# RWKV-7 chunk products merged and partly turned on VectorE, the decay inside the chunk matrices, and expert sums that start from the tokens

## What is computed

```python
def step(S, inp):                       # per head: S is 64 x 64, 8 heads, 256 steps
    r_t, w_t, k_t, v_t, a_t, b_t = inp
    sa = jnp.einsum('bhvk,bhk->bhv', S, a_t)
    S = S * w_t[:, :, None, :] + sa[..., None] * b_t[:, :, None, :] + v_t[..., None] * k_t[:, :, None, :]
    return S, jnp.einsum('bhvk,bhk->bhv', S, r_t)
...
hid = jax.nn.silu(xblk @ w_gate[e]) * (xblk @ w_up[e])      # 1024 -> 512, for each expert e
return hid @ w_down[e]                                      # 512 -> 1024
...
y = jnp.sum(yb[dest].reshape(M, TOP_K, D_) * gates[..., None].astype(yb.dtype), axis=1)
x = x + y
```

## Time and profile before

| | us |
|---|---|
| median of 3 runs | 1618.35 |
| the 3 runs | 1606.52, 1618.35, 1621.35 |
| the profiled execution: time / span | 1607.18 / 1605.4 |
| busy in the span: PE / PEld / DVE / ACT / POOL | 1159.9 / 845.2 / 357.0 / 220.8 / 84.6 |

### The profile page before, as it was taken

The page is one execution under the profiler, slowest core; times in us unless marked ns, Lnnn a source line. Parts: engine busy times, 40 slices in busy tenths (PEclk is TensorE's granted clock), DMA queues, the critical chain, the costliest instruction groups (busy, mean ns, idle before and its releaser), DMA issues.

```text
span 1605.4 us, 37750 instructions
## 1 busy us (share of the span) xinstructions
PE 1159.9 (72%) x16919; PEld 845.2 (53%) x16919; DVE 357.0 (22%) x980; ACT 220.8 (14%) x604; POOL 84.6 (5%) x132
## 2 busy tenths in 40 slices
PE   7988799898998667686656666665666666666565
PEld 4866378554786465475444444444444444444343
DVE  2455124811324514311111111111111011110111
ACT  1044012520014210210000000000000000000000
POOL 1100000000100313000000000000000000000000
PEclk9898899999997768799888888798888888888988
DMA  9740325106020002879999999999999999999997
GB/s 290 280 134 1 93 105 209 27 0 224 1 105 0 3 4 111 363 285 428 429 429 427 429 429 429 428 429 428 429 429 429 429 428 429 429 429 428 428 428 311
DMA packets 68879, 463.30 MB, mean 289 GB/s; under 512 B 14645, under 2 KB 18134, under 8 KB 44246
## 3 DMA queue, kind: packets, MB, share of 16 engines
q1 hardware_dynamic: 64784, 459.76, 69.6%
q10 hardware_dynamic: 4038, 2.69, 0.6%
HBM read 461.38 MB, written 1.05 MB: 288 GB/s over the span
## 4 chain that ended last, share of the span: by engine, by line
DMA 50%; PE 7%; DVE 1%; issue 1%; ACT 0%; POOLq 0%; SPq 0%; DVEq 0%; PEldq 0%; POOL 0%; PEld 0%
DMA weight_slots<-in_exp_w_down_dram 50%; PE bank L2096 4%; PE bank L2087 1%; PE bank L2076 1%; PE bank L2062 0%; PE bank L2055 0%; PE bank L2113 0%; DVE tokens L2285 0%; ACT work_region L2036 0%; SPq L1944 0%; DVE normed_features L2223 0%; DVE normed_tokens L2162 0%; POOLq L1979 0%; PEldq L1923 0%; DVE normed_features L2220 0%
## 5 line engine op out<-in xcount | busy, mean ns | idle before, releaser
L2087 PE MATMUL bank<-weight_slots,work_region 128*32 128x128 f32 x5504 | 200.6, 308 | 128.3 <-DMA weight_slots<-in_exp_w_up_dram 102.9
L2087 PEld LDWEIGHTS bank<-weight_slots,work_region 128*32 128x32 f32 x5504 | 173.9, 124 | 156.7 <-DMA weight_slots<-in_exp_w_up_dram 113.7
L2096 PE MATMUL bank<-weight_slots,work_region 128*32 128x256 f32 x1376 | 112.6, 482 | 90.6 <-DMA weight_slots<-in_exp_w_down_dram 90.6
L2087 PE MATMUL bank<-work_region 128*32 128x128 f32 x2688 | 97.8, 307 | 59.4 <-DMA work_region<-in_exp_w_up_dram 47.6
L2096 PEld LDWEIGHTS bank<-weight_slots,work_region 128*32 128x32 f32 x1376 | 58.1, 133 | 132.4 <-issue 91.8
L2087 PEld LDWEIGHTS bank<-work_region 128*32 128x32 f32 x2688 | 85.0, 124 | 73.2 <-DMA work_region<-in_exp_w_up_dram 53.1
L2036 ACT COPY work_region<-bank 128x256 f32<-128x256 f32 x64 | 23.9, 373 | 607.1 <-PE bank L2096 607.1
L2243 DVE TENSOR_SCALAR work_region<-work_region 128x128 f32<-128x128 f32 x128 | 38.6, 344 | 297.7 <-PE bank L2104 296.6
L2096 PE MATMUL bank<-work_region 128*32 128x256 f32 x672 | 58.8, 505 | 48.4 <-DMA work_region<-in_exp_w_down_dram 46.4
L514 PE MATMUL bank<-weight_slots,normed_features 128*128 128x512 f32 (+2 forms) x256 | 86.8, 499 | 1.9 <-DVE normed_features L700 1.9
L2254 DVE TENSOR_TENSOR work_region<-work_region,bank 128x128 f32<-128x128 f32 x64 | 23.9, 373 | 282.5 <-PE bank L2087 282.5
(11 more groups left out here) (400 smaller groups left out, 1274.6 us busy)
## 6 DMA issues: line engine op xcount, KB each, us to landing
weight_slots<-in_exp_w_up_dram SPq DMA_DIRECT2D x43, 2048.0 KB, 41.0
weight_slots<-in_exp_w_down_dram SPq DMA_DIRECT2D x43, 2048.0 KB, 40.7
weight_slots<-in_exp_w_gate_dram SPq DMA_DIRECT2D x43, 2048.0 KB, 41.7
work_region<-in_exp_w_gate_dram SPq DMA_DIRECT2D x21, 2048.0 KB, 41.7
work_region<-in_exp_w_up_dram SPq DMA_DIRECT2D x21, 2048.0 KB, 41.1
...
```

The lines of the kernel that those rows point to most:

```text
L2087: mm = nc.tensor.matmul(B[bank][BLK * j:BLK * (j + 1), 0:P], xt[u][:, c], w[u][:, c, j * P:(j + 1) * P], start=c == 0, stop=c == KC - 1, t ...
L2096: mm = nc.tensor.matmul(B[7][BLK * j:BLK * (j + 1), 0:256], hidt[u][:, BLK * k:BLK * (k + 1)], w_down[u][:, k, j * 256:(j + 1) * 256], sta ...
```

## The change

In words, and by part:

- The operands a and r now lie side by side (`reads`), so `of_features` multiplies both at once, 64 columns wide: AR takes the place of NT and RBT, KR that of AKT and RKT. N is no longer a product; VectorE transposes NT in 32 x 32 blocks.
- Of the powers, P2, P4 and P8 are formed once and VectorE transposes them. The growing sum G sits beside the powers in memory, so that `of_two` (64 columns wide) makes P4 with G's term, and P8 with G's term, in one product; G4 is alone.
- WT is a transpose on TensorE of what WU and WV hold (8 calls), where it was 64 products.
- GpSimd forms the diagonal decay matrices once; VectorE adds them to g when it takes g out of PSUM (`take_g`), so the step of the state is one product and one add. GpSimd no longer makes rk; VectorE does.
- The chunk products of tile 1 are issued chunk by chunk, between the first steps of the state. Outputs of tile 1 for the last chunk are separate.
- The expert banks begin with the tokens, by 8 products with the identity; ScalarE's zeros and VectorE's last adds go. After the last expert ScalarE and VectorE copy the banks to the tokens, and SP stores them before the engines meet.

```diff
-    ORDER = """TV0 TV1 TA0 TA1 NT0 NT1 N0 N1 AKT0 AKT1 P20 P2T0 P21 P2T1 RKT0 RKT1 F20 P40 P4T0 F21 P41 P4T1 RBT0 RBT1
-P80 F30 P81 F31 MV0 MV1 F40 F41 TK0 TK1 Q0 Q1 TB0 TB1 F50 F51 BONUS WU0 WV0 WU1 WV1 WT0 WT1 WT2 WT3""".split()
-    BY_ACT = set("TV TA P2 P2T P4 P4T P8 MV TB TK BONU WV WT".split())
+    ORDER = """TV0 TV1 TA0 TA1 AR0 AR1 KR0 KR1 P20 P21 P40 P41 P80 P81 TK0 TK1 G40 G41 MV0 MV1 Q0 Q1 TB0 TB1 F50 F51
+BONUS WU0 WV0 WU1 WV1 WT0 WT1""".split()
+    BY_ACT = set("TV TA P2 MV TK TB Q BONU WV WT".split())
...
-    pool.wait_ge(S["k_ready"], 1)
-    stepped(G.tensor_tensor(rk, r_, k_, ALU.mult))
-    G.tensor_tensor(rk, rk, shape(params[:, ROW_RK:ROW_RK + CT].unsqueeze(2), P, CT, T), ALU.mult).then_inc(S["rk_ready"], 1)
...
-    pool.wait_ge(S["scaled"], 4)
-    G.tensor_tensor(ends(ei), ends(k_), by, ALU.mult).then_inc(S["ends_ready"], 1)
     pool.wait_ge(S["scaled"], 5)
+    nc.gpsimd.tensor_tensor(ends(ei), ends(kx), by, ALU.mult).then_inc(S["ends_ready"], 1)
+    nc.gpsimd.tensor_tensor(ends(ex), ends(aa), by, ALU.mult).then_inc(S["ends_ready"], 1)
...
+    pool.wait_ge(*taken(ORDER.index("TV1")))
+    for q in range(1, NCH - 1):
+        nc.gpsimd.tensor_tensor(decay[q], shape(const("eye_head").unsqueeze(1), P, CT, HD), shape(last[:, :, q:q + 1], P, CT, HD), ALU.mult)\
+            .then_inc(S["decay_ready"], 1)
...
-    for q in range(1, NCH - 1):
-        m, c = divmod(q, 4)
-        pool.wait_ge(S["state_ready"], q)
-        stepped(G.tensor_tensor(state[:, q + 1], state[:, q], shape(last[:, :, q:q + 1], P, CT, HD), ALU.mult))
-        pool.wait_ge(S["chunk_taken"], q)
-        G.tensor_tensor(state[:, q + 1], state[:, q + 1], chunks[m][:, c, 1], ALU.add).then_inc(S["decayed"], 1)
...
+                        to = view(out[u][:, :], MT * CT, 2, CHUNK)[part(c), m * CT + i]
+                        mm = nc.tensor.matmul(to, left[half[u], i, at], reads[half[u], :, i, at], start=True, stop=True)
         mm.then_inc(S["item_made"], 2)
         made[0] += 1
...
 
+    def of_two(name, left, m, pair):
+        out = view(bank(name)[:, :], NH, 2, CHUNK)
+        for h in range(NH):
+            for c in range(4):
+                mm = nc.tensor.matmul(out[part(c), h], left[part(c), m, h], powers[part(c), pair, m, h], start=True, stop=True)
+        end(mm)
-    turn("TA0", ld, 0)
-    turn("TA1", ld, 1)
-    pe.wait_ge(S["scaled"], 3)
-    of_features("NT", aa, ld)
-    of_features("N", ld, aa)
+    turn("TA0", a_, 0)
+    turn("TA1", a_, 1)
     pe.wait_ge(S["scaled"], 4)
-    of_features("AKT", k_, ld)
-    for m in range(MT):
-        w = W[m]
-        needs("NT0", "NT1", "N0", "N1")
-        of_blocks(f"P2{m}", w["NT"], w["N"])
-        of_blocks(f"P2T{m}", w["N"], w["NT"])
+    of_features("AR", aa)
     pe.wait_ge(S["scaled"], 5)
-    of_features("RKT", k_, r_)
-    for m in range(MT):
-        w = W[m]
-        needs(f"P2{m}", f"P2T{m}")
-        pe.wait_ge(S["scaled"], 6 + m)
-        of_blocks(f"F2{m}", w["P2"], w["F"])
-        of_blocks(f"P4{m}", w["P2T"], w["P2"])
-        of_blocks(f"P4T{m}", w["P2"], w["P2T"])
-    of_features("RBT", aa, r_)
-    for m in range(MT):
-        w = W[m]
-        needs(f"P4{m}", f"P4T{m}", f"F2{m}")
-        of_blocks(f"P8{m}", w["P4T"], w["P4"])
-        of_blocks(f"F3{m}", w["P4"], w["F"])
-    for m in range(MT):
-        needs("AKT0", "AKT1", f"TV{m}")
-        of_blocks(f"MV{m}", W[m]["AKT"], view(vtok[:, m], NH, HD), HD)
-    for m in range(MT):
-        needs(f"P8{m}", f"F3{m}")
-        of_blocks(f"F4{m}", W[m]["P8"], W[m]["F"])
+    of_features("KR", kx)
+    for m in range(MT):
+        pe.wait_ge(S["n_turned"], m + 1)
+        of_blocks(f"P2{m}", NT[:, m], N[:, m])
+    for m in range(MT):
+        pe.wait_ge(S["power_turned"], m + 1)
+        pe.wait_ge(S["g_ready"], 1)
+        of_two(f"P4{m}", P2T, m, slice(0, 2))
+    for m in range(MT):
+        pe.wait_ge(S["power_turned"], MT + m + 1)
+        needs(f"P4{m}")
+        of_two(f"P8{m}", P4T, m, slice(1, 3))
     for m in range(MT):
-        w = W[m]
-        needs(f"F4{m}")
-        of_blocks(f"Q{m}", w["NO"], w["F"])
+        pe.wait_ge(S["power_turned"], 2 * MT + m + 1)
+        needs(f"P8{m}")
+        of_blocks(f"G4{m}", P8T[:, m], G[:, m])
+    for m in range(MT):
+        needs("KR0", "KR1", f"TV{m}")
+        of_blocks(f"MV{m}", AKT[:, m], view(vtok[:, m], NH, HD), HD)
+    for m in range(MT):
+        pe.wait_ge(S["no_turned"], m + 1)
+        pe.wait_ge(S["f_turned"], m + 1)
+        of_blocks(f"Q{m}", NO[:, m], F[:, m])
     pe.wait_ge(S["ends_ready"], 2)
     turn("TB0", ex, 0)
     turn("TB1", ex, 1)
     for m in range(MT):
         needs(f"Q{m}")
-        pe.wait_ge(S["xd_ready"], m + 1)
-        of_blocks(f"F5{m}", W[m]["XD"], W[m]["Q"])
-    pe.wait_ge(S["rk_ready"], 1)
+        of_blocks(f"F5{m}", G[:, m], Q[:, m])
+    pe.wait_ge(S["rk_ready"], CT)
...
-    out = []
-    for c in range(4):
-        out.append(bank(f"WT{c}"))
-        for h, i, u in HEADS:
-            for c in range(4):
-                to = slice((m * CT + i) * CHUNK, (m * CT + i + 1) * CHUNK)
-                mm = nc.tensor.matmul(out[c][half[u], to], am[part(c), m, h, 0:HD], W[m]["F"][part(c), h], start=True, stop=True)
-    mm.then_inc(S["item_made"], 4)
...
+    for m in range(MT):
+        needs(f"WU{m}", f"WV{m}")
+        out = bank(f"WT{m}")
+        for i in range(CT):
+            t = nc.tensor.transpose(out[:, i * P:(i + 1) * P], wu[:, m, 0, 2 * i:2 * i + 2].rearrange("p u d -> p (u d)"), ident)
+        end(t)
+    def chunk_products(m, some):
         for h, i, u in HEADS:
...
-                    if product == 0:
-                        nc.tensor.matmul(g_out, wu[s, m, h, 0:HD], btok[s, m, cols], start=True, stop=True)
+                    if product == 0 and 4 * m + c > 0:
+                        nc.tensor.matmul(g_out, wu[s, m, 0, h], btok[s, m, cols], start=True, stop=True)
...
-        if q == 2:
-            y_of_keys(0)
-        if q == 3:
-            pe.wait_ge(S["chunk_taken"], 5)
-            pe.wait_ge(*taken(LAST_USE[7]))
-            read_state(0)
-            y_of_state(0, range(4))
-        if q == 4:
-            pe.wait_ge(S["sa_ready"], 2)
-            y_of_writes(0)
-        if q == 5:
-            y_of_keys(1)
-        if q == 6:
-            y_of_state(1, range(3))
+    needs("TB0", "TK0")
+    for q in range(4):
+        pe.wait_ge(*taken(LAST_USE[q]))
+    chunk_products(0, range(4))
+    needs("TB1", "TK1")
+    for c in range(3):
+        pe.wait_ge(*taken(LAST_USE[4 + c]))
+        chunk_products(1, (c,))
+        if c == 0:
+            needs("KR0", "KR1", "AR0", "AR1")
+        step_state(c + 1)
+    pe.wait_ge(S["zero_state"], 1)
+    y_of_keys(0)
+    pe.wait_ge(S["g_taken"], 5)
+    pe.wait_ge(*taken(LAST_USE[7]))
+    needs("WT0", "WT1")
+    read_state(0, range(4))
+    step_state(4)
+    y_of_state(0, range(4))
+    step_state(5)
+    pe.wait_ge(S["sa_ready"], 2)
+    y_of_writes(0, range(4)).then_inc(S["y_made"], 1)
+    step_state(6)
+    y_of_keys(1)
+    read_state(1, range(3))
+    y_of_state(1, range(3))
-    read_state(1)
+    read_state(1, (3,))
     y_of_state(1, (3,))
     pe.wait_ge(S["sa_ready"], 4)
-    y_of_writes(1)
+    y_of_writes(1, range(3))
+    pe.wait_ge(S["sa_ready"], 6)
+    y_of_writes(1, (3,)).then_inc(S["y_made"], 1)
...
+    V.scalar_tensor_tensor(a_, kk, -1.0, ld, ALU.mult, ALU.mult).then_inc(S["scaled"], 1)
-    dve.wait_ge(S["rk_ready"], 1)
-    V.tensor_tensor(k_, k_, ei, ALU.mult).then_inc(S["scaled"], 1)
+    V.tensor_tensor(rx, r_, ex, ALU.mult).then_inc(S["scaled"], 1)
+    dve.wait_ge(S["k_ready"], 1)
+    V.tensor_tensor(kx, k_, ei, ALU.mult).then_inc(S["scaled"], 1)
+    dve.wait_ge(S["scaled"], 5)
+    for i in range(CT):
+        V.scalar_tensor_tensor(rk[:, i], r_[:, i], prm(ROW_RK, i), k_[:, i], ALU.mult, ALU.mult).then_inc(S["rk_ready"], 1)
...
     for u in range(2):
-        took(masked(of_half(both["NT"], u), bank(f"NT{u}"), "below_half_t"))
+        ar.append(bank(f"AR{u}"))
+        ins = masked(of_half(NT, u), pairs_of(ar[u], 0), "below_half_t")
+    after(ins)
+    for m in range(MT):
+        V.transpose(flat(N[:, m]), flat(NT[:, m])).then_inc(S["n_turned"], 1)
+    dve.wait_ge(S["n_turned"], MT)
+    V.tensor_tensor(G.rearrange("p m h b -> p (m h) b"), N.rearrange("p m h b -> p (m h) b"), shape(const("eye").unsqueeze(1), P, MT * NH, CHUNK),
+                    ALU.add).then_inc(S["g_ready"], 1)
     for u in range(2):
-        src = bank(f"N{u}")
-        masked(of_half(both["NO"], u), src, "across")
-        took(masked(of_half(both["N"], u), src, "below_half"))
-    dve.wait_ge(S["scaled"], 4)
-    V.tensor_tensor(r_, r_, ex, ALU.mult).then_inc(S["scaled"], 1)
-    for m in range(MT):
-        V.tensor_tensor(W[m]["F"], W[m]["NT"], shape(const("eye").unsqueeze(1), P, NH, CHUNK), ALU.add).then_inc(S["scaled"], 1)
+        ins = masked(of_half(NOT, u), pairs_of(ar[u], 0), "across_t")
+    after(ins)
```

(56 more changed lines are left out.)

188 lines of the change are left out of this document (99 added, 89 removed).

## The result

The changed kernel takes **1588.79 us** (median; 1582.05 to 1597.16, 4 runs) beside 1617.12 (1606.52 to 1621.35, 4 runs) for the kernel before: ratio 0.9838, 95% interval 0.98 to 0.9875. That is 28.3 us less; the prediction was 26.3 less, 1587 us, range 1572 to 1604. The profiled execution took 1582.05 with a span of 1580.3, against 1607.18 and 1605.4 before.

A forecast was written before the change was run, and what follows sets the result against it. Instruction fetch bounds PE in RWKV; the expert weight stream follows, a nearly fixed 966 us. -28.6 + 4 + 0.5 + 0.2 - 2.4 = -26.3 us, against the mean 1613.4: 1587 us, range 1572 to 1604.

The forecast's parts named there:

- Rows removed, less what the fetch no longer hides: RWKV on PE: 1032 rows fewer, 8.06 instruction blocks at 3.82 us, save 30.8 us, less 2.2 no longer hidden.
- VectorE's rk: RWKV's start: four rk pieces wait for GpSimd operations and delay the masks of AR; 4 us lost, bounds 0 and 6.5.
- Behind `y_made` and the seeding: After the last RWKV product: tile 0's norm finishes 0.5 us later; eight identity products before the ranks, 0.2 late.
- The end: After the last combine: copies on two engines and stores before the semaphore clearing move the end by -2.4 us.
- A: Rival: idle time isn't instruction count, only execution is saved; 1605, 9%. (In "from A": start of the transposes of V.).
- B: Rival in RWKV: the chain of round trips (product, copy, turn, next product) binds instead; gain 20.4 us, 1593; 16%.
- C: Rival in the expert loop: TensorE's clock stays at the lower level throughout, losing 55 us; slower, 1642; 4%.
- D: Rival: the gain comes, but the router's gap grows by what PE or VectorE lose there; 1594; 6%.

The follow-up runs named there:

- chunk products first: The changed kernel with all chunk products of tile 1 ahead of the first three state steps, not between them: 1585.87 us.
- rk late: The changed kernel with VectorE's four pieces of rk moved later in its queue, behind the block transposes of F; run twice: 1583.3 and 1582.1 us.
- the two kernels on the old code: The kernel before with F5 computed three times, 1621.38 us; the kernel before with every 32-wide block product made 64 wide, 1612.52 us.

## Why the prediction was right

**Right in its mechanism.** The time came out 2 us from the forecast, and its reason is shown and not only argued: two blocks of instructions more cost 6.7 us, wider rows nothing, and the waits on "issue" fell from 25.6 to 6.9 us where I had said that I was wrong if they stayed at 26. The stream of the experts followed the first load as said: 965 to 969 us in all ten profiles, whose first loads lie between 601.8 and 640.8.

**Rows removed, less what the fetch no longer hides: -28.6.** The two profiles with rk out of the way have 70.65 us from A to first load, the two with the old RWKV 99.17: -28.5. In part that is luck: it is a sum of two errors that cancel. To the chunk products I had laid out 43.9 us (530.8 to 574.7) and these two measure 42.7. From the chunk products to the first load I had -1.6 and found -0.5. PE there is held for 8 us at clock 0.50 without an idle moment (the first window above), while the fetch had set the pace in the plan; that fewer rows save little where half-clock products fill the block's time is how I read it, no run takes it apart.

**VectorE's rk: +4, bounds 0 and 6.5.** The four changed profiles with rk in front average 74.4 us from A to first load, the two with it behind 70.65: 3.8 (3.4 without the kernel with chunk products first). The picture was right too: the masks came 6.7 us after AR's products, where I had 5 to 8 (539 to 542 in place of 534), and 2.9 of the 6.7 were made good. The first profile of the changed kernel alone, 72.03, would have said 1.4: P4 and P8 (L1453) took 5.9 us of PE there and the next blocks came 3.7 and 3.4 us apart; in its second profile they took 6.6, and the blocks came 4.0 and 3.9 us apart. Both had WU and WV (L1509) at granted clock 1.00, 3.70 us, where both runs with rk late had them at 0.67, 5.36 us, and so lost 1.7 us of their lead; but the kernel without seeds had 5.36 with rk in front. The clock is as large as what is compared here. The whole times agree in size (1583.3 and 1582.1 beside 1588.79 and 1589.05), but the ratios' intervals, 0.981 and 0.9824 beside 0.9838 and 0.9822, overlap; by them alone the gain of rk late is not shown.

**Behind `y_made` and the seeding: +0.5 and +0.2.** The seeds were mis-sized: on the changed kernel the gap is 1.2 us shorter with them. They took 3.67 us there, where I had 5.0, and the five pairs of ranks behind them 1.3 in place of 2.4, on the kernel before as well; there logits at half clock took the gain away. -1.2 and -0.2 (37.0 in place of 37.2) are inside my range of -2.4 to +2. What I did not have at all is the 1.9 us more of the router's gap: logits, gather and gate products at a higher clock, for which the cause stays open. The 0.5 us for the norm can't be told: first to ninth load took 22.8 us before and 23.2 after, but 23.5 to 25.8 in the other eight profiles, of both kinds. Of the 3.1 us only 1.1 arrive at the last combine: from tenth load to last combine it is 907.9 us in the changed kernel, 906.3 before.

**The end: -2.4, bounds -1 and -3.4.** Measured -1.6 in the changed kernel's first profile, -2.5 in the second, -2.1 with the seeds and stores alone. Right, and confirmed by undoing it (8.6, and 6.5 to 7.4 with it). The whole times give the seeds and stores together more than my -2.2: 8 us on the kernel before (4 to 13), and 4 to 7 on the changed one (ratio 0.9865 without them, 0.9838 and 0.9822 with them, intervals that overlap). By them RWKV alone has 21 us (17 to 27) of my 24.1. The stretches don't show this, and it stays open; the sum is better borne out than the shares of its terms.

**Upstream.** The sum began at the profiled execution before, whose A was at 530.82; the profiled execution after had 535.71. I could not foresee this; it is chance, as the ten values of A show, and it is why the RWKV part won 27.3 and the profiled times differ by only 25.1. Taking the mean of the four executions as the base, 1613.4, was what brought the forecast to 1587; from the median shown, 1618.35, the same sum gives 1592, 3 us on the other side of what was measured. The two pairs of executions, 1607 and 1620, that I saw were chance as well: the 19 runs of this kernel beside the one with more products lie between 1604.23 and 1623.8 with no gap over 4 us, and the mean I took is near their median, 1614.05.

**The rivals.** A fell with the two kernels on the old code. B (1593) shows in two waits for VectorE, 4.57 and 1.58 us, and they were rk and not the round trips: with rk late PE waits for no engine but its sequencer until WT's copy, 0.7 us. C didn't come: clock 0.85 in the loop. D came with the opposite sign: the router's gap was 3.1 us shorter, not 7 longer.

On one rule page and traces differ. The Trainium skill ("Runtime: NRT & Kernel Launch", Instruction fetch mechanics) calls the fetch of blocks "mostly hidden". The traces here show it in the open for rows of 15 ns, with 25.6 us idle beside 27.0 busy, and 256 rows more cost 6.7 us; where the rows are 128 columns wide (L1509), or 64 wide at a granted clock near 0.50 (the 3.8 us for 128 rows), it is indeed hidden.
